# Expert-numbered blocks, early weight loads into slots of their own, and a permuted row order in a mixture-of-experts layer

## The chip, the cores and the metric

The kernel is one program on one core of a Trainium2 chip. The metric is device time in microseconds (us) for one execution; the smaller, the better.

## What is computed

One encoder layer on a sequence of 1024 tokens of width 1024, all in float32. A convolutional mixer comes first, then a mixture of experts (MoE) with 32 experts in 4 groups of 8. Each token takes the best group, then the two best experts in it, which makes 2048 pairs of token and expert. Cut to what matters here:

```python
order = jnp.argsort(expert)                      # 2048 pairs, sorted by expert
counts = jnp.bincount(expert, length=N_EXPERTS)
padded = ((counts + BLOCK_ROWS - 1) // BLOCK_ROWS) * BLOCK_ROWS     # BLOCK_ROWS = 128
...
def expert_block(args):
    xblk, e = args                               # 128 rows of width 1024
    a = xblk @ w_gate[e]                         # 1024 x 512
    u = xblk @ w_up[e]                           # 1024 x 512
    return (jax.nn.silu(a) * u) @ w_down[e]      # 512 x 1024
...
yb = yb * w_buf[:, None].astype(yb.dtype)
out = jnp.zeros_like(xt).at[tok_buf].add(yb)
```

With the inputs of the reference, the routing gives every expert between 10 and 130 tokens. One expert alone has more than 128, so there are 33 blocks, with 62 filled rows each on average.

## The kernel before

The engines run their own programs and meet at semaphores. TensorE (PE) multiplies. ScalarE (ACT) and VectorE (DVE) split each float32 operand into a high and a low part (`_hi`, `_lo`), and a product is three matmuls (`three`). GpSimd (POOL) issues the indirect transfers, and SyncE (SP) issues the weight loads.

**Routing.** After the output projection, DVE works out the experts, the weights, and for each pair its block and its row in the block. `posf` is the pair's place in the padded order. `blkf` is that place divided by 128 and `rowf` the rest. A one-hot product on PE (`inverse`, from `inv_b` and `oh_r`) turns this into the token of each row of each block, `idx_all`. `oh_r` compares `rowf` with `iota_r`, so partition p of a block holds row `iota_r[p]`, which is row p here. An unfilled row gets an index out of bounds, and the indirect transfers skip it. `tab` holds the expert of each block and the number of blocks, `n_blk`. `s_tab` says that `tab` is ready, and `s_pos` that `idx_all` is.

**Weights.** A block needs 6 chunks of 1024 KB: four of gate and up (a load of 512 KB of each, `load_gu`) and two of down (`load_down`). `e_raw`, `e_hi` and `e_lo` have one place for each of the six chunks. ACT rounds `e_raw` to `e_hi`, then DVE subtracts to get `e_lo` (semaphores `gu_lo`, `d_lo`), and then the place in `e_raw` is free for the next load. SP issues in this order: gate and up of block b+2, chunk by chunk as `gu_lo` of block b+1 arrives, then down of block b+1 as `d_lo` of block b arrives:

```python
e_gu = expert_of(b + 2)
for q in range(4):
    held(gu_lo, b * 4 + (4 + q + 1))
    load_gu(q, e_gu)
...
e_down = expert_of(b + 1)
for q in range(2):
    held(d_lo, b * 2 + (q + 1))
    load_down(q, e_down)
```

The loads of block 0 are issued behind the last matmul of the output projection (`pe_o`), and those of block 1 behind `s_tab`, the value that it gives, and `gu_lo` of block 0. A load has landed when its semaphore has had an increment from each of the DMA engines.

**A block.** POOL gathers the filled rows of the block from `d_h2` in HBM to `xg`, 4 KB each, two blocks ahead. PE transposes them, ACT and DVE split them (`xT_hi`, `xT_lo`), and PE multiplies by gate and up in 48 matmuls of 512 columns. ACT and DVE make `hid`, PE transposes it, and PE multiplies by down in 24 more matmuls. DVE scales the result to `y_sb` (L1389 in the profile, once a block). POOL adds the filled rows onto `d_x1` in HBM by an indirect transfer with accumulation (L632). The last two blocks go a way of their own, through a one-hot product and `f_x`.

**Tail.** SP loads `f_x`, DVE adds and norms, and the output is stored.

## Time and profile before

| what | before |
|---|---|
| median of 3 runs | 1692.61 us (1691.16 to 1692.96) |
| the profiled execution's own time | 1691.49 us |
| its span | 1689.8 us |
| mean granted clock of PE | 0.983 |
| busy: PE, PE weight load, DVE, ACT, POOL | 94%, 76%, 81%, 41%, 22% |
| moved by DMA | 351.83 MB, mean 208 GB/s |

The span is from the first to the last instruction of the profiled execution. The busy shares are means over stages that have different limits. From 1060.8 us to 1655.4 us the kernel is in the expert blocks, and what the change touches lies there and in the 80 us ahead of it. PE's busy time is modelled from pipelined matmuls, so an idle stretch of PE is surer than a busy one. The DMA share is the mean busy share of the 16 DMA engines.

### The profile page before, as it was taken

Reading aid. Unit: us, or ns where it says so; the run is one execution under the profiler, and the core shown is the slowest. Engines: PE = TensorE matmul, PEld = TensorE weight load, DVE = VectorE, ACT = ScalarE, POOL = GpSimd, SP = SyncE. Lnnn points to the kernel's source line nnn. Section 1 sums busy time; section 2 is a strip of 40 time slices with the busy share of each in tenths; the row PEclk is TensorE's granted clock in tenths of the full one; section 3 lists DMA queues with packets and bytes.
Section 4 is the critical chain, followed back from the end, with each engine's and each line's share of the span. In section 5 each row is a group of like instructions: output and inputs, shape, how many; then the busy total and the mean of one; then the engine's idle time right before and its main releaser. Section 6 shows DMA issues by size and latency. Waiting matters only on the chain.

```text
span 1689.8 us, 21438 instructions
## 1 busy us (share of the span) xinstructions
PE 1584.6 (94%) x7093; PEld 1291.7 (76%) x7093; DVE 1360.3 (81%) x1151; ACT 695.4 (41%) x584; POOL 365.5 (22%) x217
## 2 busy tenths in 40 slices
PE   2699999999999999999999988999999999999985
PEld 2588888888888888778878856888887777777774
DVE  5777878697878877988465467999999989989996
ACT  3411011211112012346131135777777666666773
POOL 1101000000000010000000011455454544445451
PEclk9999999999999999999999969999999999999997
DMA  7414233232314233535453248999999999999964
GB/s 251 151 63 137 63 111 105 73 120 87 112 62 137 58 116 114 179 118 187 140 174 138 87 175 310 367 364 372 377 357 351 355 359 358 356 351 359 371 198 163
DMA packets 167196, 351.83 MB, mean 208 GB/s; under 512 B 16907, under 2 KB 90659, under 8 KB 167158
## 3 DMA queue, kind: packets, MB, share of 16 engines
q1 hardware_dynamic: 150888, 309.73, 51.6%
q0 software_dynamic: 16272, 41.62, 8.1%
q8 instruction: 22, 0.36, 0.1%
q14 instruction: 14, 0.11, 0.0%
HBM read 323.32 MB, written 45.62 MB: 218 GB/s over the span
## 4 chain that ended last, share of the span: by engine, by line
PE 61%; DMA 16%; DVE 12%; issue 5%; ACT 3%; POOL 1%; DVEq 0%; SPq 0%; POOLq 0%; ACTq 0%
PE ps L1483 19%; PE ps L1485 19%; PE ps L1484 19%; DMA e_raw<-in_w_down_dram 12%; DMA xg<-d_h,g_idx 3%; DVE e_lo L1368 2%; DVE e_lo L1364 2%; ACT e_hi L854 2%; DVE conv_acc_b L1094 1%; DVE macc L1000 1%; PE ps L1703 1%; POOL g_idx L626 1%; PE ps L1636 1%; DVE B_lo L1179 1%; DMA prow<-in_c_dram 1%
## 5 line engine op out<-in xcount | busy, mean ns | idle before, releaser
L1483 PE MATMUL ps<-A_hi,w_hi 128*128 128x512 f32 x1024 | 400.7, 391 | 4.7 <-DVE A_lo L1030 4.7
L1485 PE MATMUL ps<-A_hi,w_lo 128*128 128x512 f32 x1024 | 399.3, 390 | 0.0
L1484 PE MATMUL ps<-A_lo,w_hi 128*128 128x512 f32 x1024 | 399.3, 390 | 0.0
L1364 DVE TENSOR_TENSOR e_lo<-e_raw,e_hi 128x2048 fp32r<-128x2048 f32 x136 | 309.1, 2286 | 11.5 <-ACT e_hi L848 9.9
L1094 DVE SCALAR_TENSOR_TENSOR conv_acc_b<-glu,colc,conv_acc_b 128x1024 f32<-128x1024 f32 x232 | 298.0, 1284 | 10.2 <-DVE rows L1079 0.5
L848 ACT CAST e_hi<-e_raw 128x2048 fp32r<-128x2048 f32 x136 | 259.7, 1913 | 61.3 <-PE ps L1485 56.6
L1483 PEld LDWEIGHTS ps<-A_hi,w_hi 128*128 128x128 f32 x1024 | 192.8, 188 | 46.0 <-issue 4.4
L1484 PEld LDWEIGHTS ps<-A_lo,w_hi 128*128 128x128 f32 x1024 | 192.8, 188 | 40.4 <-issue 0.5
L1485 PEld LDWEIGHTS ps<-A_hi,w_lo 128*128 128x128 f32 x1024 | 192.7, 188 | 40.2
L1483 PE MATMUL ps<-e_hi,xT_hi 128*128 128x512 f32 x528 | 212.5, 403 | 0.0
L1485 PE MATMUL ps<-e_hi,xT_lo 128*128 128x512 f32 x528 | 207.0, 392 | 0.0
L1484 PE MATMUL ps<-e_lo,xT_hi 128*128 128x512 f32 x528 | 206.3, 391 | 0.0
L1368 DVE TENSOR_TENSOR e_lo<-e_raw,e_hi 128x2048 fp32r<-128x2048 f32 x66 | 150.7, 2285 | 28.4 <-ACT e_hi L854 28.4
L854 ACT CAST e_hi<-e_raw 128x2048 fp32r<-128x2048 f32 x66 | 126.0, 1911 | 92.2 <-DMA e_raw<-in_w_down_dram 67.7
L632 POOL DMA_INDIRECT d_x<-y_sb,s_idx x31 | 86.4, 2786 | 297.2 <-DVE y_sb L1389 286.1
L970 DVE TENSOR_TENSOR w_lo<-w_raw,w_hi 128x1024 fp32r<-128x1024 f32 x72 | 87.9, 1222 | 63.9 <-ACT w_hi L711 60.4
L711 ACT CAST w_hi<-w_raw 128x1024 fp32r<-128x1024 f32 x72 | 73.6, 1047 | 156.8 <-PE ps L1485 154.0
L1483 PE MATMUL ps<-e_hi,hT_hi 128*128 128x512 f32 x264 | 106.6, 404 | 10.5 <-DVE hT_lo L1383 10.4
L1485 PEld LDWEIGHTS ps<-e_hi,xT_lo 128*128 128x128 f32 x528 | 99.4, 188 | 21.7
L1483 PEld LDWEIGHTS ps<-e_hi,xT_hi 128*128 128x128 f32 x528 | 100.1, 190 | 18.6
L1484 PEld LDWEIGHTS ps<-e_lo,xT_hi 128*128 128x128 f32 x528 | 99.7, 189 | 18.9
L1484 PE MATMUL ps<-e_lo,hT_hi 128*128 128x512 f32 x264 | 105.1, 398 | 0.0
(286 smaller groups left out, 2113.6 us busy)
## 6 DMA issues: line engine op xcount, KB each, us to landing
e_raw<-in_w_gate_dram SPq DMA_DIRECT2D x132, 512.0 KB, 6.0
e_raw<-in_w_up_dram SPq DMA_DIRECT2D x132, 512.0 KB, 12.5
e_raw<-in_w_down_dram SPq DMA_DIRECT2D x66, 1024.0 KB, 14.0
w_raw<-in_w_in_dram SPq DMA_DIRECT2D x56, 512.0 KB, 4.2
stream<-in_w_ada_dram SPq DMA_DIRECT2D x48, 512.0 KB, 5.6
xn<-in_x_dram SPq DMA_DIRECT2D x8, 512.0 KB, 6.5
d_short<-conv_acc_a POOLq DMA_DIRECT2D x8, 512.0 KB, 4.0
d_gate_a<-gate_st POOLq DMA_DIRECT2D x8, 512.0 KB, 2.9
```

What stands on the lines that cost most here:

```text
L626: g.tensor_copy(g_idx[:, slot:slot + 1], idx_all[:, bass.ds(blk, 1)]).then_inc(p_copy, 1)
L632: g.indirect_dma_start(d_x1, bass.IndirectOffsetOnAxis(ap=idx_ap, axis=0), rows_ap, None, bounds_check=S - 1, oob_is_err=False, compute_op ...
L711: a.copy(w_hi[:, slot, :], w_raw[:, slot, :]).then_inc(w_hi_done, 1)
L848: a.copy(e_hi[:, q, :], e_raw[:, q, :]).then_inc(gu_hi, 1)
L854: a.copy(e_hi[:, 4 + q, :], e_raw[:, 4 + q, :]).then_inc(d_hi, 1)
L970: v.tensor_tensor(w_lo[:, slot, :], w_raw[:, slot, :], w_hi[:, slot, :].bitcast(F32), ALU.subtract).then_inc(w_lo_done, 1)
L1094: lstep(v.scalar_tensor_tensor(conv_acc_b[:], glu[:, t:t + S], w, conv_acc_b[:], ALU.mult, ALU.add))
L1364: v.tensor_tensor(e_lo[:, q, :], e_raw[:, q, :], e_hi[:, q, :].bitcast(F32), ALU.subtract).then_inc(gu_lo, 1)
L1368: v.tensor_tensor(e_lo[:, 4 + q, :], e_raw[:, 4 + q, :], e_hi[:, 4 + q, :].bitcast(F32), ALU.subtract).then_inc(d_lo, 1)
L1483: t.matmul(dst, st_hi, mv_hi, start=first, stop=False)
L1484: t.matmul(dst, st_hi, mv_lo, start=False, stop=False)
L1485: return t.matmul(dst, st_lo, mv_hi, start=False, stop=last)
```

## The change

It has four parts.

1. **Block numbers.** Block e, for e from 0 to 31, is the first 128 rows of expert e. Rows past 128 of an expert go to blocks 32 and up. An expert's blocks past the first are now counted from `cmp_nb[:, 1:NT]`. `own` (the pair's expert) and the block past 32 make `blkf`. `n_blk` is 32 plus the blocks past the first, 33 as before for these inputs. DVE does more for this, in another order.
2. **Early weights.** Since blocks 0 to 31 need no table, SP issues gate and up of block 1 right behind block 0's, into four places of their own (`park`: the two down places of `e_hi`, one of `e_lo`, and two rows of `rows`). Gate and up of block 2 go to `e_raw` when block 0 has been split, and down of block 1 when block 0's has. The loop of SP starts at b = 1. ACT and DVE read block 1's chunks from `park`.
3. **Order on DVE.** The four splits of block 0 are no longer cut in two by `x_lo` of block 0.
4. **Row order.** `iota_r` is permuted. Partitions 0 to 3 hold rows 0, 16, 32 and 48, partitions 4 to 7 rows 1, 17, 33 and 49, and so on: partition 64h + 32a + 4b + c holds row 8h + 64a + b + 16c. Partitions 0 to 31 and 64 to 95 thus hold the first 64 rows.

The diff, cut to its core:

```diff
+        park = [at("park0", (NCH + 4) * 4 * C8, [P, C8], F32), at("park1", (NCH + 5) * 4 * C8, [P, C8], F32),
+                at("park2", (2 * NCH + 5) * 4 * C8, [P, C8], F32), at("park3", oR + SH2 * T4, [P, C8], F32)]
...
-            def load_gu(q, e):
+            def load_gu(q, e, parked=False):
                 for part, w in ((0, w_gate), (1, w_up)):
-                    dst = e_raw[:, q, part * D:(part + 1) * D].rearrange("p (k n) -> p k n", k=2)
+                    raw = park[q] if parked else e_raw[:, q, :]
+                    dst = raw[:, part * D:(part + 1) * D].rearrange("p (k n) -> p k n", k=2)
                     src = w[bass.ds(e, 1), 2 * q * P:2 * (q + 1) * P, :].rearrange("a (p k) n -> p (a k) n", p=P)
-                    sp.dma_start(dst, src).then_inc(e_full[q], 16)
+                    sp.dma_start(dst, src).then_inc((park_full if parked else e_full)[q], 16)
...
-            sp.wait_ge(s_tab, 1)
-            n_blk = sp.value_load(tab[0:1, NBLK:NBLK + 1], min_val=PAIRS // P, max_val=NBLK - 1)
-            e_one = sp.value_load(tab[0:1, 1:2], min_val=0, max_val=NE - 1)
+            for q in range(2):
+                load_gu(q, 1, True)
+            sp.wait_ge(s_h2, NT)
+            load_gu(3, 1, True)
+            sp.wait_ge(s_lgev, NT)
+            sp.wait_ge(sp_h2, 16 * NT)
+            load_gu(2, 1, True)
             for q in range(4):
                 sp.wait_ge(gu_lo, q + 1)
-                load_gu(q, e_one)
-            with sp.Fori(0, NBLK) as b:
+                load_gu(q, 2)
+            for q in range(2):
+                sp.wait_ge(d_lo, q + 1)
+                load_down(q, 1)
+            sp.wait_ge(s_tab, 1)
+            n_blk = sp.value_load(tab[0:1, NBLK:NBLK + 1], min_val=NE, max_val=NBLK - 1)
+            with sp.Fori(1, NBLK) as b:
...
-            g.iota(iota_r[:], pattern=[[1, P]], base=0, channel_multiplier=0, allow_small_or_imprecise_dtypes=True)
+            for half in range(2):
+                g.iota(iota_r[:, half * P // 2:(half + 1) * P // 2].rearrange("p (a b c) -> p a b c", a=2, b=8), pattern=[[P // 2, 2], [1, 8], [P // 8, 4]],
+                       base=half * 8, channel_multiplier=0, allow_small_or_imprecise_dtypes=True)
...
+            both = [P, 2, NT, NE]
+
+            def of_pair(dst, per_expert):
+
+                step(v.tensor_tensor(big[:], e_k[:], per_expert, ALU.mult))
+                step(v.tensor_reduce(dst, big[:], AX_X, ALU.add))
+
+            of_pair(own[:], bc(iota_n[:].unsqueeze(1), both))
...
-            step(v.tensor_reduce(nb_e[:], cmp_nb[:], AX_X, ALU.add))
+            step(v.tensor_reduce(nb_e[:], cmp_nb[:, 1:NT], AX_X, ALU.add))
...
+            rank = ps[:, 0, 0:NT * NE].rearrange("p (i e) -> p i e", i=NT)
+            of_pair(posf[:], bc(rank.unsqueeze(1), both))
+            step(v.tensor_copy(posi[:], posf[:]))
+            step(v.tensor_scalar(blk_i[:], posi[:], P.bit_length() - 1, None, ALU.arith_shift_right))
+            step(v.tensor_copy(blkf[:], blk_i[:]))
+            step(v.scalar_tensor_tensor(rowf[:], blkf[:], -float(P), posf[:], ALU.mult, ALU.add))
+            dve.wait_ge(h2_free, NT)
...
+            of_pair(posf[:], bc(cum[:, 0, :].unsqueeze(1).unsqueeze(1), both))
+            step(v.tensor_tensor(posf[:], posf[:], blkf[:], ALU.add))
+            step(v.scalar_tensor_tensor(posf[:], posf[:], float(NE - 1), own[:], ALU.add, ALU.subtract))
+            step(v.tensor_scalar(blkf[:], blkf[:], 1.0, None, ALU.min))
+            step(v.tensor_tensor(posf[:], posf[:], blkf[:], ALU.mult))
+            step(v.tensor_tensor(blkf[:], posf[:], own[:], ALU.add))
...
+            step(v.tensor_scalar(tab[:, NBLK:NBLK + 1], over, float(NE), None, ALU.add))
+            step(v.tensor_scalar(tab[:, NBLK + 1:NBLK + 2], over, float(NE - 1), None, ALU.add))
+            v.scalar_tensor_tensor(tab[:, 0:NBLK], ps[0:1, 1, H:H + NBLK], float(NE - 1), blk_own[0:1, :], ALU.min,
+                                   ALU.add).then_inc(s_tab, 1)
...
             n_blk = dve.value_load(tab[0:1, NBLK:NBLK + 1], min_val=PAIRS // P, max_val=NBLK - 1)
-            for q in range(2):
+            for q in range(4):
                 gu_split(q, q + 1)
             x_lo(0, 1)
-            for q in range(2, 4):
-                gu_split(q, q + 1)
 
             x_lo(1, 2, 1)
             for q in range(3):
-                gu_split(q, 4 + q + 1)
+                gu_split(q, 4 + q + 1, True)
             hidden(0, 1)
-            gu_split(3, 8)
+            gu_split(3, 8, True)
+            dve.wait_ge(gu_lo, 8)
```

The rows of `order` below name an instruction by its line, its operation and its tiles.

DVE between the counts of the experts and the first one-hot (`inv_b`), before. `nb_b` is what PE multiplies into the block starts, and `cum<-ps` reads them:

```order
L1309 TENSOR_TENSOR cnt_e<-ps,ident 32x1
...
L1312 TENSOR_SCALAR nb_b<-ones,nb_e 32x128
L1317 COPY cum<-ps 128x32
L1318 SCALAR_TENSOR_TENSOR mask<-cum,ps 128x256
L1321 TENSOR_TENSOR e_k<-e_k,mask 128x256
L1322 TENSOR_REDUCE posf<-e_k 128x8
...
L1323 CAST posi<-posf 128x16
L1326 TENSOR_SCALAR blk_i<-posi 128x16
L1327 CAST blkf<-blk_i 128x16
L1328 SCALAR_TENSOR_TENSOR rowf<-blkf,posf 128x16
L1330 TENSOR_TENSOR inv_b<-blk_no,blkf 128x8x48
```

The same place after the change:

```order
L1335 TENSOR_TENSOR big<-e_k,iota_n 128x512
L1336 TENSOR_REDUCE own<-big 128x16
L1340 TENSOR_TENSOR cnt_e<-ps,ident 32x1
...
L1343 TENSOR_SCALAR nb_b<-ones,nb_e 32x128
L1335 TENSOR_TENSOR big<-e_k,ps 128x512
L1336 TENSOR_REDUCE posf<-big 128x16
...
L1351 SCALAR_TENSOR_TENSOR rowf<-blkf,posf 128x16
L1356 COPY cum<-ps 128x32
L1335 TENSOR_TENSOR big<-e_k,cum 128x512
L1336 TENSOR_REDUCE posf<-big 128x16
L1358 TENSOR_TENSOR posf<-posf,blkf 128x16
...
L1362 TENSOR_TENSOR blkf<-posf,own 128x16
L1364 TENSOR_TENSOR inv_b<-blk_no,blkf 128x8x48
```

One pair of operations on 512 elements now stands ahead of `cnt_e`, one between `nb_b` and `cum<-ps`, and one behind it with five small operations.

SP, the weight loads from the last down chunk of block 0 to its loop, before:

```order
L475 DMA e_raw<-in_w_down_dram 128x2x1024 x2
L486 TENSOR_LOAD tab
...
L471 DMA e_raw<-in_w_gate_dram 128x1024
L471 DMA e_raw<-in_w_up_dram 128x1024
...
L491 UNCONDITIONAL_BRANCH
```

and after the change (`park_163` to `park_166` are the four places, chunks 0 to 3):

```order
L482 DMA e_raw<-in_w_down_dram 128x2x1024 x2
L478 DMA park_163<-in_w_gate_dram 128x1024
...
L478 DMA park_166<-in_w_gate_dram 128x1024
...
L478 DMA park_165<-in_w_gate_dram 128x1024
L478 DMA park_165<-in_w_up_dram 128x1024
L478 DMA e_raw<-in_w_gate_dram 128x1024
...
L482 DMA e_raw<-in_w_down_dram 128x2x1024 x2
L506 TENSOR_LOAD tab
```

The loads of block 1 moved ahead of the reading of the table, and those of block 2 and the down chunks of block 1 moved out of the loop and ahead of it too.

## Rows read from the trace of the kernel before

**Rows 1.** The page's slices of the span, 42.2 us each: DMA share and rate.

```profile
DMA  7414233232314233535453248999999999999964
GB/s 251 151 63 137 63 111 105 73 120 87 112 62 137 58 116 114 179 118 187 140 174 138 87 175 310 367 364 372 377 357 351 355 359 358 356 351 359 371 198 163
```

**Rows 2.** Busy time of each engine in stretches of the span.

```profile
core 0: us, PE busy (x) PEld busy (x) DVE busy (x) ACT busy (x) POOL busy (x), PEclk, DMA share, GB/s
980.00:990.00 10.00, 7.57 (x16) 3.66 (x16) 8.66 (x29) 1.63 (x3) 1.04 (x2) 0.50 1.01 404
...
994.00:1011.00 17.00, 12.09 (x46) 9.44 (x47) 11.75 (x36) 3.49 (x2) 0.00 (x0) 0.52 0.00 0
1011.00:1061.00 50.00, 41.97 (x177) 32.04 (x176) 40.21 (x24) 26.77 (x19) 8.52 (x7) 0.93 0.80 297
1060.00:1243.00 183.00, 182.12 (x846) 148.96 (x845) 176.58 (x111) 133.70 (x91) 95.56 (x40) 1.00 1.01 368
1243.00:1589.00 346.00, 329.50 (x1513) 265.73 (x1512) 316.31 (x200) 239.02 (x163) 161.36 (x72) 1.00 1.00 356
1589.00:1643.00 54.00, 51.91 (x240) 42.61 (x239) 52.94 (x34) 40.85 (x28) 30.73 (x13) 1.00 0.70 242
```

**Rows 3.** Line 1389, once a block, in three stretches; first and last start.

```profile
L1389 DVE SCALAR_TENSOR_TENSOR y_sb<-ps,w_all,rows x11: 1275/1278/1279, 1060.8 to 1243.3; 128x1024 f32<-128x1024 f32 x11
...
L1389 DVE SCALAR_TENSOR_TENSOR y_sb<-ps,w_all,rows x19: 1276/1278/1280, 1243.3 to 1588.9; 128x1024 f32<-128x1024 f32 x19
...
L1389 DVE SCALAR_TENSOR_TENSOR y_sb<-ps,w_all,rows x4: 1276/1277/1278, 1588.9 to 1642.9; 128x1024 f32<-128x1024 f32 x4
```

**Rows 4.** Waits, 1060 to 1240 us (first row), 1250 to 1590 us (others).

```profile
ACT e_hi L854 <- DMA e_raw<-in_w_down_dram: 3.8, 3, 1.4
...
ACT e_hi L854 <- DMA e_raw<-in_w_down_dram: 61.5, 33, 3.6
...
PE ps L1703 <- DMA xg<-d_h,g_idx: 11.6, 15, 1.3
```

**Rows 5.** Median time from issue to landing, 1050 to 1160, then 1250 to 1400 us.

```profile
e_raw<-in_w_down_dram SPq DMA_DIRECT2D x12, 1024.0 KB, 9.9
...
e_raw<-in_w_down_dram SPq DMA_DIRECT2D x16, 1024.0 KB, 14.6
```

**Rows 6.** The page: GpSimd's queue (packets, MB, share of 16 engines), and DMA issues.

```profile
q0 software_dynamic: 16272, 41.62, 8.1%
...
e_raw<-in_w_up_dram SPq DMA_DIRECT2D x132, 512.0 KB, 12.5
e_raw<-in_w_down_dram SPq DMA_DIRECT2D x66, 1024.0 KB, 14.0
...
d_short<-conv_acc_a POOLq DMA_DIRECT2D x8, 512.0 KB, 4.0
```

**Rows 7.** Timeline of DVE, 988 to 1003 us: start, duration, idle before in brackets.

```profile
988.65 0.88 DVE L1295 TENSOR_TENSOR e_k<-oh_g,oh_k 128x256 f32<-128x256 f32 x2 [0.15 <-DVE gsm L1291]
...
994.29 0.15 DVE L1309 TENSOR_TENSOR cnt_e<-ps,ident 32x1 f32<-32x1 f32 x1 [1.41 <-PE ps L1675]
...
995.97 0.19 DVE L1317 COPY cum<-ps 128x32 f32<-128x32 f32 x1 [0.78 <-PE ps L1678]
...
999.31 0.56 DVE L1330 TENSOR_TENSOR inv_b<-blk_no,blkf 128x384 f32<-128x384 f32 x1
...
1001.08 1.22 DVE L1334 TENSOR_TENSOR oh_r<-iota_r,rowf 128x1024 f32<-128x1024 f32 x1
```

**Rows 8.** Timelines of PE and of ACT at the start of the blocks.

```profile
1023.24 1.98 PE L1703 MATMUL ps<-ident,xg 128*128 128x128 f32 x8 [1.88 <-DMA xg<-d_h,idx_all]
...
1029.18 1.91 ACT L848 CAST e_hi<-e_raw 128x2048 fp32r<-128x2048 f32 x1 [2.91 <-PE ps L1485]
```

**Rows 9.** Timeline of POOL where it makes its constants, 880 to 886 us.

```profile
881.79 0.24 POOL L598 IOTA iota_r<- 128x128 f32 x1
...
885.11 0.55 POOL L607 DMA_DIRECT2D d_x<-stream  x1 [2.80 <-DVE stream L1234]
```

More of the change, by code:

```diff
@@ L186, in encoder_block @@
         blk_no = rt("blk_no", [P, NBLK])
+        blk_over = rt("blk_over", [P, NBLK])
+        blk_own = rt("blk_own", [P, NBLK])
+        iota_n = rt("iota_n", [P, NT, NE])
         gsm = rt("gsm", [P, 8, NT])
@@ L205, in encoder_block @@
         blk_i = rt("blk_i", [P, 2, NT], I32)
+        own = rt("own", [P, 2, NT])
         blkf = rt("blkf", [P, 2, NT])
@@ L208, in encoder_block @@
         tok1 = rt("tok1", [P, NT])
-        inv_b = rt("inv_b", [P, 2, NT, 2, NBLK])
         oh_r = at("oh_r", oW, [P, 2, NT, P], F32)
         iota_r = rt("iota_r", [P, P])
+        inv_b = rt("inv_b", [P, 2, NT, 2, NBLK])
         no_row = rt("no_row", [P, NBLK])
@@ L512, in _ @@
             sp.wait_ge(s_oht, 4)
-            sp.dma_start(rows[:, SH2, :], g_final.partition_broadcast(P).rearrange("p a n -> p (a n)")).then_inc(s_g2_in, 16)
+            sp.dma_start(rows[:, GT1, :], g_final.partition_broadcast(P).rearrange("p a n -> p (a n)")).then_inc(s_g2_in, 16)
             for i in range(NT):
@@ L684, in _ @@
                 pool.wait_ge(f_norm, n + 1)
-                g.tensor_tensor(f_o[:, i, :], f_n[:, n % 2, :], rows[:, SH2, :], ALU.mult).then_inc(f_outp, 1)
+                g.tensor_tensor(f_o[:, i, :], f_n[:, n % 2, :], rows[:, GT1, :], ALU.mult).then_inc(f_outp, 1)
         @block.scalar
@@ L1317, in _ @@
             step(v.tensor_copy(cum[:, 0, :], ps[:, 3, 0:NE]))
-            step(v.scalar_tensor_tensor(mask[:], bc(cum[:, 0, :].unsqueeze(1), [P, NT, NE]), float(P),
-                                        ps[:, 0, 0:NT * NE].rearrange("p (i e) -> p i e", i=NT), ALU.mult, ALU.add))
-            for k in range(2):
-                step(v.tensor_tensor(e_k[:, k], e_k[:, k], mask[:], ALU.mult))
-                step(v.tensor_reduce(posf[:, k, :], e_k[:, k], AX_X, ALU.add))
-            step(v.tensor_copy(posi[:], posf[:]))
-            dve.wait_ge(h2_free, NT)
-            step(v.tensor_scalar(blk_i[:], posi[:], P.bit_length() - 1, None, ALU.arith_shift_right))
-            step(v.tensor_copy(blkf[:], blk_i[:]))
-            step(v.scalar_tensor_tensor(rowf[:], blkf[:], -float(P), posf[:], ALU.mult, ALU.add))
+            of_pair(posf[:], bc(cum[:, 0, :].unsqueeze(1).unsqueeze(1), both))
[4 more added lines that the diff above has]
+            step(v.tensor_tensor(blkf[:], posf[:], own[:], ALU.add))
             for k in range(2):
@@ L1463, in final @@
                     if i not in POOL_TILES:
-                        v.scalar_tensor_tensor(f_o[:, i, :], f_x[:, i, :], rstd[:, i:i + 1], rows[:, SH2, :],
+                        v.scalar_tensor_tensor(f_o[:, i, :], f_x[:, i, :], rstd[:, i:i + 1], rows[:, GT1, :],
                                                ALU.mult, ALU.mult).then_inc(f_out, 1)
```

47 lines of the change are left out of this document (25 added, 22 removed).

## Prediction

> **What bounds the kernel now.** I read the slices first. From slice 26 to 38 the DMA share stands at its top digit and the rate at 351 to 377 GB/s, with no great rise or fall [rows 1]. That covers the expert blocks, and it does not say who waits for whom. The stretches do [rows 2]. From 1060 to 1243 us PE is busy 182.12 of 183 us, so PE sets the pace there, although the DMA share reads 1.01. From 1243 to 1589 us it is busy 329.50 of 346 us, while the rate has gone down from 368 to 356 GB/s at the same share. The line that ends a block shows the pace [rows 3]: (1243.3 - 1060.8)/10 = 18.25 us a block, then (1588.9 - 1243.3)/18 = 19.20 us, then (1642.9 - 1588.9)/3 = 18.0 us.
>
> The waits name what changed [rows 4]. ACT waits for the down chunks 3.8 us in the first stretch and 61.5 us in the second. A down load takes 9.9 us to land early and 14.6 us later [rows 5]. So the weight stream runs a little slower than PE from the start. It lives on a reserve of some 5 to 8 us in the time to landing, which ten blocks eat up at about 1 us a block. From then on the stream is the bound.
>
> What makes the stream slow? A block's weights are 4 x 2 x 512 KB and 2 x 1024 KB, that is 6.29 MB [rows 6]. At the 404 GB/s that the same loads reach at 980 to 990 us [rows 2] they need 15.6 us. The rest of the 19.2 us is 3.6 us for 62 rows of 4 KB in and as many out. These are 0.51 MB, 1.3 us at that rate when all 16 engines share them equally. GpSimd's queue took 8.1% of 16 engines' span, 8.1% x 16 x 1689.8 = 2190 us of engine time, for 41.62 MB [rows 6]. Of these, 48 plain stores of 512 KB (six groups of eight, one of which is shown) are 25.2 MB, 997 us at 404/16 GB/s for each engine. That leaves 1193 us, or 36 us for each of 33 blocks. Over 16 engines it is 2.3 us, over 8 engines 4.5 us. So a block costs 17.8 us on every engine if the rows are spread evenly, and 20.1 us on the loaded ones if half of the engines carry them. The measured 19.2 us is nearer to the second. Filled rows lie in partitions 0 to 61 on average, half of the 128, so I take it that half of the engines carry them and that every weight load, which needs its last engine, waits for these.
>
> No row tells the engine of a packet. The Trainium skill ("DMA: Bandwidth & Descriptors", The descriptor swizzle) gives engine = 8 x (partition >> 6) + ((partition >> 2) & 7) for a transfer over 128 partitions. By it, partitions 0 to 63 are engines 0 to 7, and the new order puts row r on engine r mod 16; that no row here can show, and 19.2 us agrees with it.
>
> **The change, part by part.**
>
> *Row order.* The same rows now load all engines. With the 3.6 us as the pace of eight loaded engines, the rows are 29 us of engine time, 1.8 us on each of 16, and a block's stream takes 15.6 + 1.8 = 17.4 us. The bound from the queue's share is 17.8 us. Both are under PE's 18.25 us, so the weights should leave the path and the 18 slow blocks should run at 18.25 us: 18 x 0.95 = 17.1 us gained. The first ten and the last three blocks gain nothing, since PE holds them already. As a check, the idle time of PE from 1243 to 1643 us is 16.5 + 2.1 = 18.6 us, of which 1.9 us stay at the first stretch's 0.5%: 16.7 us. The margin of 0.45 to 0.85 us a block is thin, and blocks are unequal (10 to 128 rows). I leave 1.0 us of waits standing. If the margin is not there, the price is 0.1 us x 18 for each 0.1 us above 18.25, after the reserve is gone.
>
> *Early weights.* The DMA engines are idle from 994 to 1011 us (share 0.00) and at 0.80 from 1011 to 1061 us [rows 2]. Four MB of block 1 move into the first gap. But nobody waited for them: at 1029.18 us, when ACT begins with block 1, it has waited for PE [rows 8]. The gain can only be a larger reserve for later. At block 1 the reserve is nearly whole already, since a down load takes 9.9 us in the median of the first six blocks. Bounds: 0 at one end, and at the other the transfer of 4.19 MB at 356 GB/s, 11.8 us, if the stream were the bound without a break from 1033 us on. Where the row order takes the stream off the path, it is 0, which I take. Where it doesn't, I take 1.9 us, two blocks at the 0.95 us by which the slow ones are slower: nearer to 0, since the reserve is used up only some ten blocks later.
>
> *Routing on DVE.* The edits from `cnt_e` to `inv_b` are on the path, for PE waits for the one-hots. An operation on 256 elements takes 0.44, on 384 elements 0.56 and on 1024 elements 1.22 us [rows 7]. So one on 512 is about 0.70, and a pair is 1.4 us. The first pair (`own`) goes into the 1.41 us in which DVE waited for the counts: nothing. Without that cover it would cost 1.4 us. Then from the end of `nb_b`, before: 0.78 us of waiting, and 3.34 us from `cum` at 995.97 to `inv_b` at 999.31, together 4.1 us. After: 1.4 + four small operations at 0.2 + `cum` 0.2 + 1.4 + five small 1.0 = 4.9 us. The block starts have arrived by then. The sum is +0.8 us, and `s_tab` and `s_pos` move with it. Behind them stand the gathers, SP's table and every engine's `n_blk`.
>
> *First gathers.* PE starts block 0 after the rows of block 1, for which it waits 1.88 us until 1023.24 us [rows 8]. With the rows spread, these gathers should land somewhat sooner, beside 2 MB of weight loads as before. Bounds 0 and 1.0 us; I take 0.5 us, half of it, since I have no row of a spread gather.
>
> *POOL's constants.* Five more small operations (`iota_r` is made in two halves) come between 881.79 and 885.11 us. At the 0.24 us of `iota_r` they are some 1.2 us in all, and POOL has 2.80 us there [rows 9]: nothing. Four splits of block 0 in a row on DVE: PE reads them later than DVE ends them in both orders, nothing. DVE's and ACT's added waits are for their own or finished work, nothing. The number of blocks stays 33, and the tail after 1643 us is the same work.
>
> **Sum,** against the profiled execution's own 1691.49 us: -17.1 + 1.0 + 0.8 - 0.5 = -15.8, so 1675.7 us. The median of the runs is 1.1 us above that execution, which makes 1676.8 us; I say 1677.
>
> **Rivals.**
>
> 1. *The stream stays the bound, halfway.* The share reads 1.00 to 1.01 in both stretches [rows 2], as if all 16 engines were busy and none had room for the others' rows. For it: that reading. Against it: at the same share the rate is 404, 368 and 356 GB/s, so the share does not tell work from standing in line. If the evened pace is 18.7 us, half of the gain is left: 18 x 0.5 = 9.0 and 1.9 from the early weights, less 0.3 of routing and gathers and 2 for unequal blocks: 8.6 us, about 1684 us.
> 2. *The rows cost what they cost on any engine, or the partitions are dealt to engines in another way than I take.* Then the new order changes nothing, the late blocks stay at 19.2 us, and the early weights give 1.9 us, less 0.3 us of routing and gathers: 1691 us. For it: the share again, and no row with an engine's number. Against it: 3.6 us for what at an even deal costs 1.3 to 2.3 us. The Trainium skill (same page, Specifications) gives about 358 GB/s as HBM's limit for one core, which speaks against this change: by it 356 GB/s is the end and 1691 us the outcome. The trace does not agree, with 368 GB/s over 183 us and 404 GB/s over 10 us.
> 3. *Slower: sixteen late engines instead of eight.* Each load waits for its last engine. If scattering with accumulation holds up whichever engine it is on, all 16 now have it, and the last of 16 is later than the last of 8, from the first block on. At 19.2 us for all 31 periods the first ten cost 9.5 us more: 1692.6 + 9.5 + 0.3 = 1702 us. It decides from a mean period of 18.8 us on. For it: the longest wait ends with a load, not a row. Against it: the work on each engine halves, and the first ten blocks already run at 18.25 us with such scatters. The Trainium skill (same page, Latency and other measured facts) says that engines 7 and 15 are usually slower than the others; engine 15 would now get rows as well. No run here shows engines apart.
>
> **How the numbers follow.** My forecast has 0.66, rival 1 has 0.16, rival 2 has 0.12, rival 3 has 0.06. The forecast's own range is 1672 us (gathers and PE's waits fully gained) to 1680 us (pace 18.4 us). With rival 1 and the near edge of rival 2 the range is 1671 to 1690 us. A change under 0.2%, 3.4 us, is about what a measurement of this kernel can't tell from none. Rival 2 falls within it, with a part of rival 1's upper end: faster 0.83, same 0.11, slower 0.06.
>
> **What the changed kernel's profile would show.** The line that ends a block comes every 18.2 to 18.4 us throughout, also from 1243 us on. ACT's wait for down chunks stays under 15 us over all blocks, and the time to landing stays near 10 us. PE is busy over 98% from 1060 to 1620 us. `inv_b` starts 0.8 us later. There is a burst of DMA between 994 and 1011 us, and the first matmul of block 0 starts at 1025 us as before. I am wrong if the late blocks keep 19.2 us (rival 2) or stop between (rival 1), or if the first ten lose their 18.25 us (rival 3).

## The result, and the profile after

The changed kernel takes 1670.7 us (median of 4 runs, 1668.35 to 1673.36), the kernel before on the same chip 1692.78 us (4 runs, 1691.16 to 1694.01). The ratio is 0.9871 with a 95% interval from 0.9854 to 0.9888: 22.1 us faster. The forecast was 1677.0 us in a range from 1671 to 1690. The direction was right, and the time is 6.3 us below the forecast and 0.3 us below the range. The profiled execution took 1670.95 us, with a span of 1669.3 us, against 1691.49 and 1689.8 us.

From the page of the changed kernel: the slices of the span (41.7 us each), GpSimd's queue and the issues of the weight loads, as in [rows 1] and [rows 6].

```profile
DMA  7414133232323142544544273999999999999964
GB/s 254 153 64 137 50 127 97 79 113 95 116 66 113 63 139 54 198 151 139 172 155 156 101 288 140 329 369 394 374 358 391 377 373 368 378 386 382 375 195 167
q0 software_dynamic: 16272, 41.88, 8.3%
e_raw<-in_w_down_dram SPq DMA_DIRECT2D x66, 1024.0 KB, 7.6
e_raw<-in_w_up_dram SPq DMA_DIRECT2D x128, 512.0 KB, 7.1
```

The same work of GpSimd's queue is there (16272 packets, and its share is about the same), yet the weights land in 7.6 and 7.1 us where it was 14.0 and 12.5 us [rows 6]. The rate in the expert blocks is 358 to 394 GB/s, where it was 351 to 377 [rows 1].

Busy time of the engines in the stretches of [rows 2], for the changed kernel:

```profile
core 0: us, PE busy (x) PEld busy (x) DVE busy (x) ACT busy (x) POOL busy (x), PEclk, DMA share, GB/s
980.00:990.00 10.00, 7.08 (x16) 3.20 (x15) 8.63 (x30) 1.69 (x3) 1.29 (x2) 0.62 1.02 412
994.00:1011.00 17.00, 11.06 (x45) 9.04 (x45) 12.79 (x38) 3.44 (x2) 0.00 (x0) 0.50 0.55 220
1011.00:1061.00 50.00, 43.32 (x172) 32.27 (x172) 40.24 (x26) 25.41 (x18) 6.99 (x7) 0.91 0.58 215
1060.00:1243.00 183.00, 183.00 (x860) 151.57 (x859) 178.84 (x113) 136.38 (x92) 93.83 (x40) 1.00 1.00 371
1243.00:1589.00 346.00, 343.95 (x1601) 282.55 (x1600) 335.37 (x210) 253.73 (x171) 181.34 (x76) 1.00 1.01 377
```

The early weights show as a share of 0.55 from 994 to 1011 us, where the DMA engines were idle. From 1243 to 1589 us PE is idle for 2.05 us instead of 16.5. The DMA share reads 1.01 there at 377 GB/s, where it read 1.00 at 356 [rows 2]: the share is the same, and the bytes are 6% more.

The line that ends a block (1425 now, 1389 before), over the same blocks as in [rows 3]:

```profile
L1425 DVE SCALAR_TENSOR_TENSOR y_sb<-ps,w_all,rows x11: 1276/1278/1279, 1061.6 to 1241.7; 128x1024 f32<-128x1024 f32 x11
...
L1425 DVE SCALAR_TENSOR_TENSOR y_sb<-ps,w_all,rows x19: 1276/1277/1278, 1241.7 to 1568.6; 128x1024 f32<-128x1024 f32 x19
...
L1425 DVE SCALAR_TENSOR_TENSOR y_sb<-ps,w_all,rows x4: 1276/1276/1278, 1568.6 to 1622.9; 128x1024 f32<-128x1024 f32 x4
```

That is 18.01 us a block for the first ten (before 18.25), 18.16 us for the next 18 (before 19.20) and 18.1 us for the last three (before 18.0).

The waits from 1243 to 1589 us hold no down chunk any more, against 61.5 us in [rows 4]. What is left for a transfer is this row, 11.6 us before:

```profile
PE ps L1738 <- DMA xg<-d_h,g_idx: 2.0, 6, 0.6
```

The routing on DVE, for the rows of [rows 7]:

```profile
992.73 0.69 DVE L1335 TENSOR_TENSOR big<-e_k,iota_n 128x512 f32<-128x512 f32 x1
993.46 0.69 DVE L1336 TENSOR_REDUCE own<-big 128x16 f32<-128x512 f32 x1
994.24 0.14 DVE L1340 TENSOR_TENSOR cnt_e<-ps,ident 32x1 f32<-32x1 f32 x1
...
997.55 0.19 DVE L1356 COPY cum<-ps 128x32 f32<-128x32 f32 x1
...
1000.27 0.56 DVE L1364 TENSOR_TENSOR inv_b<-blk_no,blkf 128x384 f32<-128x384 f32 x1
```

The pair for `own` lies where DVE waited 1.41 us for the counts, and `cnt_e` starts at 994.24 us as before (994.29). `inv_b` starts at 1000.27 instead of 999.31 us.

The starts of PE and ACT that answer to [rows 8]:

```profile
1023.33 1.98 PE L1738 MATMUL ps<-ident,xg 128*128 128x128 f32 x8 [1.94 <-DMA xg<-d_h,idx_all]
```

```profile
1028.91 1.91 ACT L870 CAST e_hi<-park 128x2048 fp32r<-128x2048 f32 x1 [2.55 <-PE ps L1520]
```

PE waits for the rows of block 1 as it did, 1.94 us, and is 0.1 us later although the routing is 1.0 us later.

### The profile page after: what moved, and what is told of

The parts are those of the page before. It is cut to its first block, busy times and chain, and to the rows that moved or that the text cites. A ratio compares the mean times of both kernels' runs of the same rounds, so it can differ in the third digit from the quotient of the medians.

```text
span 1669.3 us, 21394 instructions
## 1 busy us (share of the span) xinstructions
PE 1580.0 (95%) x7093; PEld 1293.9 (78%) x7093; DVE 1364.7 (82%) x1157; ACT 697.0 (42%) x584; POOL 374.5 (22%) x222
## 3 DMA queue, kind: packets, MB, share of 16 engines
q0 software_dynamic: 16272, 41.88, 8.3%
## 4 chain that ended last, share of the span: by engine, by line
PE 80%; DVE 8%; issue 4%; DMA 4%; ACT 2%; POOL 1%; DVEq 0%; POOLq 0%; SPq 0%; ACTq 0%
PE ps L1518 25%; PE ps L1520 25%; PE ps L1519 25%; DMA xg<-d_h,g_idx 3%; PE ps L1738 2%; DVE macc L1023 1%; ACT e_hi L870 1%; DVE e_lo L1400 1%; POOL g_idx L648 1%; PE ps L1743 1%; PE ps L1671 1%; DVE B_lo L1202 1%; DMA prow<-in_c_dram 0%; DVE xnT L1010 0%; PE ps L1720 0%
## 5 line engine op out<-in xcount | busy, mean ns | idle before, releaser
L1400 DVE TENSOR_TENSOR e_lo<-e_raw,e_hi 128x2048 fp32r<-128x2048 f32 x132 | 301.2, 2287 | 15.4 <-ACT e_hi L870 14.2
L870 ACT CAST e_hi<-e_raw 128x2048 fp32r<-128x2048 f32 x132 | 251.9, 1912 | 80.5 <-PE ps L1520 80.5
L1404 DVE TENSOR_TENSOR e_lo<-e_raw,e_hi 128x2048 fp32r<-128x2048 f32 x66 | 150.6, 2283 | 0.9 <-ACT e_hi L876 0.9
L876 ACT CAST e_hi<-e_raw 128x2048 fp32r<-128x2048 f32 x66 | 126.1, 1913 | 47.7 <-PE ps L1520 47.7
L1520 PE MATMUL ps<-e_hi,hT_lo 128*128 128x512 f32 x264 | 105.5, 400 | 0.0
```

The costliest lines, as they stand in the source:

```text
L870: a.copy(e_hi[:, q, :], park[q][:] if parked else e_raw[:, q, :]).then_inc(gu_hi, 1)
L876: a.copy(e_hi[:, 4 + q, :], e_raw[:, 4 + q, :]).then_inc(d_hi, 1)
L1400: v.tensor_tensor(e_lo[:, q, :], park[q][:] if parked else e_raw[:, q, :], e_hi[:, q, :].bitcast(F32), ALU.subtract).then_inc(gu_lo, 1)
L1404: v.tensor_tensor(e_lo[:, 4 + q, :], e_raw[:, 4 + q, :], e_hi[:, 4 + q, :].bitcast(F32), ALU.subtract).then_inc(d_lo, 1)
L1520: return t.matmul(dst, st_lo, mv_hi, start=False, stop=last)
```

## The experiments

Two theories were to be told apart first. Theory A: the rows' place is the whole gain, because the weight stream leaves the path; the early weights add nothing. Theory B: the early weights are part of it. When the first runs had answered that, the size of the gain and the first ten blocks were still open.

All runs, with the ratio to the kernel before on the same chip. A block's time is the distance of the starts of the line that ends a block, as in [rows 3], for the first ten, the next 18 and the last three. The measurement tells 0.2% (3.4 us) from no change.

| run | us, median | ratio, 95% interval | us a block |
|---|---|---|---|
| before | 1692.8 | 1 | 18.25, 19.20, 18.0 |
| after | 1670.7 | 0.9871 [0.9854, 0.9888] | 18.01, 18.16, 18.1 |
| e1 rows only | 1670.07 | 0.987 [0.9855, 0.9885] | 18.11, 18.04, 18.0 |
| e2 early weights only | 1693.57 | 1.0013 [1.0004, 1.0022] | 18.27, 19.19, 17.7 |
| e3 even engines | 1679.8 | 0.9935 [0.9917, 0.9953] | 18.12, 18.54, 17.7 |
| e8 odd engines | 1681.64 | 0.9941 [0.9917, 0.9964] | 18.28, 18.58, 17.7 |
| e9 pairs in both halves | 1682.05 | 0.9943 [0.9928, 0.9959] | 18.11, 18.59, 17.7 |
| e10 upper half | 1692.94 | 1.0008 [0.9997, 1.0019] | 18.22, 19.12, 18.0 |
| e4 before, half of the down bytes | 1679.11 | 0.9932 [0.9913, 0.995] | 18.32, 18.42, 18.1 |
| e7 e4 and gather first | 1667.17 | 0.9859 [0.9835, 0.9883] | 17.97, 17.93, 17.9 |
| e6 before and gather first | 1689.76 | 0.9992 [0.998, 1.0004] | 18.25, 19.23, 17.7 |
| e5 after and gather first | 1667.07 | 0.9855 [0.9832, 0.9877] | 17.96, 17.93, 17.9 |
| e11 rows only and gather first | 1665.59 | 0.9841 [0.9827, 0.9854] | 17.97, 17.93, 17.9 |

### One part at a time: rows only (e1), early weights only (e2)

e1 is the kernel before with one edit, e2 the changed kernel with this edit undone.

```diff
-            g.iota(iota_r[:], pattern=[[1, P]], base=0, channel_multiplier=0, allow_small_or_imprecise_dtypes=True)
+            for half in range(2):
+                g.iota(iota_r[:, half * P // 2:(half + 1) * P // 2].rearrange("p (a b c) -> p a b c", a=2, b=8), pattern=[[P // 2, 2], [1, 8], [P // 8, 4]],
+                       base=half * 8, channel_multiplier=0, allow_small_or_imprecise_dtypes=True)
```

> The kernel before with the new row order alone: block numbers, early weights and DVE's routing as before. Theory A (the spread rows are the whole gain, the rest costs about 0.8 us of routing): 1669 to 1673 us, blocks at 18.0 us early and 18.2 us late, like the changed kernel or up to 1 us better. Theory B (the early weights give a reserve that the spread alone lacks): 1675 to 1683 us, late blocks at 18.5 us or more. Theory C (the early weights are the gain): 1690 us or more.

> The changed kernel with the old row order (partition p holds row p): early weights and expert-numbered blocks alone. Theory A: 1690 to 1694 us, early blocks at 18.2 us, late ones at 19.2 us. Theory B: the larger reserve puts off the slow stretch by a few blocks, 1684 to 1689 us. Theory C: 1671 to 1676 us.

e1 took 1670.07 us, what the changed kernel takes. Its waits from 1243 to 1589 us hold no down chunk, and this row is what is left for a transfer:

```profile
PE ps L1705 <- DMA xg<-d_h,g_idx: 0.7, 3, 0.3
```

e2 took 1693.57 us, nothing gained and, by its interval, 0.04 to 0.22% lost, which has room for the routing's 1 us. In the profile of e2 the down chunks are waited for as before, and a little more than before:

```profile
ACT e_hi L874 <- DMA e_raw<-in_w_down_dram: 66.4, 35, 4.0
```

So one table of 128 numbers is the gain. And the 4 MB in the gap, with the new numbers of the blocks that make them possible, bring nothing that can be told from noise, with spread rows and without.

### Is it the load on each engine? Four other placements (e3, e8, e9, e10)

Each has other numbers in `iota_r`, with all the rest of the changed kernel. The engines named are by a rule of the Trainium skill ("DMA: Bandwidth & Descriptors", The descriptor swizzle), which deals the partitions in groups of four, 0 to 63 to engines 0 to 7 and 64 to 127 to engines 8 to 15. No run here shows an engine's number.

In this order, e3 (partition 8m + s holds row m + 16s: the even engines), e8 (rows 0 to 63 in every second group of four partitions: the odd engines) and e10 (rows 0 to 63 in partitions 64 to 127):

```diff
+            g.iota(iota_r[:].rearrange("p (m s) -> p m s", s=8), pattern=[[1, 16], [16, 8]], base=0, channel_multiplier=0,
+                   allow_small_or_imprecise_dtypes=True)
...
+            for s in range(2):
+                g.iota(iota_r[:].rearrange("p (m s c) -> p m s c", m=16, s=2)[:, :, s, :], pattern=[[1, 16], [16, 4]], base=64 * (1 - s),
+                       channel_multiplier=0, allow_small_or_imprecise_dtypes=True)
...
+            g.iota(iota_r[:, 0:P // 2], pattern=[[1, P // 2]], base=P // 2, channel_multiplier=0, allow_small_or_imprecise_dtypes=True)
+            g.iota(iota_r[:, P // 2:P], pattern=[[1, P // 2]], base=0, channel_multiplier=0, allow_small_or_imprecise_dtypes=True)
```

e9 (adjacent pairs of engines in both halves):

```diff
+            for h in range(2):
+                for a_ in range(2):
+                    for y in range(2):
+                        part = iota_r[:, h * 64 + a_ * 32:h * 64 + a_ * 32 + 32].rearrange("p (x y z) -> p x y z", x=2, y=2)
+                        g.iota(part[:, :, y, :].rearrange("p x (z c) -> p x z c", z=2), pattern=[[2, 2], [1, 2], [8, 4]],
+                               base=64 * y + 4 * h + 32 * a_, channel_multiplier=0, allow_small_or_imprecise_dtypes=True)
```

It puts rows 0 to 63 into the first eight of every 16 partitions: 0-7, 16-23, 32-39 and so on to 112-119. By the rule these are the engines that the expectation below names, 0, 1, 4, 5, 8, 9, 12 and 13; the partitions that it names are wrong.

> The changed kernel with another permuted order: partition 8m+s holds row m+16s, so a block of 64 rows fills partitions 0-3 of each group of 8. If an engine serves 8 neighbouring partitions (0 to 7, 8 to 15, ...), this spreads rows over all 16 engines and gives 1670 us like the changed kernel. If an engine serves two groups of 4 neighbours, 32 apart, as the Trainium skill (DMA: Bandwidth & Descriptors, The descriptor swizzle) has it, the rows again lie on 8 engines, and it gives 1688 to 1694 us with late blocks at 19.2 us. If it is not about engines at all but about any permutation of partitions, 1670 us.

> The changed kernel with another row order: rows 0 to 63 in partitions 4-7, 12-15, 20-23 and so on, the other half of each group of eight. By the Trainium skill (DMA: Bandwidth & Descriptors, The descriptor swizzle) these are engines 1, 3, 5 to 15, where the order that gave 1679.8 us used engines 0, 2, 4 to 14. Theory P (it matters how the eight engines are spread over the sixteen): 1678 to 1682 us again. Theory S (it matters whether one of two slower engines, 7 and 15, carries rows): 1688 to 1694 us, as with the old order, which has engine 7 among its eight.

> The changed kernel with other numbers in iota_r alone: a block's first 64 rows stand in partitions 0-15, 32-47, 64-79 and 96-111, by the page's rule on engines 0, 1, 4, 5, 8, 9, 12, 13: eight engines again, in adjacent pairs, but half of them in each half of the sixteen. Both earlier placements on every other engine (one on the even, one on the odd ones) took some 1680-1682 us, the placement on engines 0-7 took 1693.6. Theory N (engines 2k and 2k+1 share something, so that two loaded neighbours hold each other up): as on engines 0-7, 1690 to 1694 us, slow blocks at 19.2. Theory H (it matters that rows load one half of the engines, 0-7, and not the other): as every other engine, 1678 to 1683 us, slow blocks at 18.5. In between would mean that neither alone is the cause.

> The changed kernel with iota_r turned by 64: a block's first 64 rows stand in partitions 64-127, by the page's rule on engines 8-15 alone. Theories N (neighbours) and H (one half of the sixteen) both expect the time of the old order: 1690 to 1695 us, slow blocks at 19.2. If engines 0-7 had other work besides (small loads, stores of few rows) that made them the late ones, these engines would be better: under 1688 us. If engine 15 were slow, worse: over 1697 us.

e3 fitted none of its expectations, and e8 was made for the first explanation of that, which fell: the odd engines, 7 and 15 among them, take 1681.64 us, where the even ones take 1679.8. The Trainium skill (same page, Latency and other measured facts) says that 7 and 15 are usually the slow ones; no run here shows it. e9 and e10 then separated neighbours from halves. Eight loaded engines in one half cost 1693 us, lower or upper alike; in e10 ACT's waits for down chunks are nearly those of before:

```profile
ACT e_hi L875 <- DMA e_raw<-in_w_down_dram: 57.3, 33, 3.7
```

Eight loaded engines in both halves cost 1680 to 1682 us, neighbours or not. All sixteen cost 1670.

Two things outside of the profile's own views, taken from its record of each engine's completions, show what happens. "spread" is the time from the eighth to the last of the 16 engines' completions of a block's first down chunk:

```
us from block to block, blocks 1 to 31
before 17.7 18.8 18.0 18.5 18.1 17.9 18.1 18.2 18.3 19.0 19.1 19.3 19.5 17.5 19.2 19.5 19.4 18.8 19.9 18.8 20.7 18.3 20.3 19.2 19.4 18.6 19.2 18.9 17.8 18.4 17.8
e3     18.5 18.2 17.9 18.2 17.9 17.9 18.3 18.3 18.0 17.9 17.9 18.0 18.1 18.2 18.3 18.7 18.1 18.3 18.3 18.3 18.8 20.0 18.3 19.9 18.4 17.5 18.9 19.8 17.5 17.7 17.9
after  18.2 17.9 18.1 17.9 17.9 17.9 18.2 17.9 17.9 17.9 17.9 17.9 18.0 18.0 17.9 17.9 17.9 18.5 18.9 18.5 18.2 18.5 17.9 18.4 18.2 17.9 18.3 17.9 18.5 17.9 17.9
spread, us, blocks 0 to 30
before 1.2 1.7 1.6 1.0 2.1 4.3 3.9 3.7 5.9 6.1 7.0 8.8 9.4 9.3 10.2 7.4 8.5 9.6 10.0 8.5 9.1 9.2 11.3 9.0 10.6 9.6 9.5 8.8 9.1 8.8 5.9
e3     1.5 0.2 0.3 0.9 2.0 2.2 3.0 4.0 2.9 3.3 1.8 1.5 1.8 4.7 4.9 3.4 3.6 5.0 4.5 5.7 5.1 7.2 8.0 9.4 8.3 8.6 8.6 7.0 7.1 9.6 5.8
after  1.4 0.3 0.3 1.1 0.5 2.3 2.7 2.4 1.2 2.1 1.4 1.8 1.3 2.3 1.2 0.6 1.6 1.2 1.8 1.2 1.0 1.6 1.7 2.8 1.8 1.8 1.1 0.8 0.7 2.1 2.7
```

Before, the last engine falls behind from block 5 on until it is some 9 us behind the eighth, where it stays. From then on the blocks take 19.2 us. In e3 the same happens at about half the speed, so that its last blocks are nearly as slow as those of before, and fewer. After, the last stays within 3 us of the eighth. All 16 completions tell how many engines are late:

```
us behind the first engine, in the order in which they end: first down chunk, mean of blocks 20 to 28
before 0.0 0.0 0.1 0.1 0.2 0.2 0.3 0.4 0.8 0.9 1.5 1.7 2.2 2.9 5.2 10.0
e10    0.0 0.0 0.1 0.2 0.2 0.2 0.3 0.8 1.1 1.3 1.5 1.9 2.2 2.6 6.3 10.0
e3     0.0 0.0 0.1 0.1 0.2 0.3 0.4 1.0 2.6 2.8 3.3 3.5 6.8 7.8 8.1 8.7
e8     0.0 0.1 0.1 0.2 0.3 0.4 0.5 0.9 2.3 2.4 2.8 3.0 3.3 5.9 8.7 9.1
e9     0.0 0.1 0.1 0.2 0.3 0.4 0.5 0.8 2.3 2.4 2.5 3.6 4.9 5.5 7.8 9.0
after  0.0 0.1 0.2 0.2 0.3 0.3 0.4 0.5 0.7 0.8 1.0 1.2 1.3 1.5 1.8 1.9
```

Before and in e10 one engine is far behind and a second half as far. In e8 two or three are late, in e3 and e9 four. It is never eight alike.

So the load on each engine decides, as the prediction took it. Placements on eight engines differ by 11 to 13 us, and it looks as if the eight of one half shared something. But e3, e8 and e9 differ from before and e10 in a second thing, which none of the expectations reckons with: how evenly the eight are loaded. Blocks are unequal, and in the order of before and e10 a block is filled from its first partition on, so a block of 33 rows gives engine 0 five rows and engines 1 to 7 four each. e3, e8 and e9 deal the rows to their engines in turn. From the counts of the experts in the reference's inputs (33, 34, 66, 111 rows in the first four blocks) and the rule above, the rows of the most loaded engine over all 33 blocks are these:

| placement | most loaded | the next three | us |
|---|---|---|---|
| before, e2; e10 (8 to 15) | 237 | 228, 222, 216 | 1692.8, 1693.57; 1692.94 |
| e3, e8 | 221 | 217, 214, 212 | 1679.8, 1681.64 |
| e9 | 218 | 215, 211, 208 | 1682.05 |
| after, e1 | 145 | 141, 138, 136 | 1670.7, 1670.07 |

It fits that before and e10 have one engine far behind, with 9 rows more than the next, and that e3, e8 and e9 have two to four close together, with 9 or 10 rows between the first and the fourth, where before has 21. As an estimate, the prediction's 1193 us of engine time for 2048 rows in and out is 0.58 us a row, so 16 to 19 rows more on the engine that every load waits for are 9 to 11 us, of the 11 to 13 measured. That leaves little or nothing for something shared by the engines of a half. It is argued and not shown: no run deals the rows in turn to the engines of one half.

### How fast without the stream? Half of the down bytes (e4, e7)

```diff
-                src = w_down[bass.ds(e, 1), 2 * q * P:2 * (q + 1) * P, :].rearrange("a (k p) n -> p (a k) n", p=P)
-                sp.dma_start(e_raw[:, 4 + q, :].rearrange("p (k n) -> p k n", k=2), src).then_inc(e_full[4 + q], 16)
+                n_k = 2 if isinstance(e, int) else 1
+                src = w_down[bass.ds(e, 1), 2 * q * P:(2 * q + n_k) * P, :].rearrange("a (k p) n -> p (a k) n", p=P)
+                sp.dma_start(e_raw[:, 4 + q, 0:n_k * D].rearrange("p (k n) -> p k n", k=n_k), src).then_inc(e_full[4 + q], 16)
```

This is the kernel before with the second half of each down chunk left out from block 1 on. It computes with a stale half. A block's weights are 5.24 MB instead of 6.29.

> The kernel before, with only the first half of each down chunk loaded from block 1 on (512 instead of 1024 KB; the other half keeps old data, so the second half of each down product is left to stale weights). All instructions stay. It takes 1 MB of 6.3 MB a block from the stream. Theory A (18.25 us in the first ten blocks was not PE's own pace, the stream cost something there too): all blocks at 17.9 to 18.0 us, 1662 to 1672 us. Rival (18.25 us is PE's pace): first ten blocks stay at 18.2 to 18.3 us, and the rest come down to that, 1674 to 1677 us.

e4 took 1679.11 us: more than the changed kernel with all of its bytes, which no theory expected. Its profile has no wait for weights, and the DMA share has room for the first time:

```profile
1060.00:1243.00 183.00, 180.59 (x842) 148.52 (x842) 176.10 (x111) 133.65 (x90) 93.81 (x40) 1.00 0.89 306
1243.00:1589.00 346.00, 340.40 (x1582) 278.80 (x1581) 331.26 (x207) 251.04 (x170) 169.27 (x76) 1.00 0.92 315
```

The waits of that run from 1243 to 1589 us that have to do with the rows' transposes:

```profile
PEld ps L1704 <- issue: 11.0, 13, 1.3
PE ps L1704 <- DMA xg<-d_h,g_idx: 5.3, 8, 0.9
```

So with the stream out of the way there was a second thing at 18.3 to 18.4 us a block, and it is not PE's own work. The gathers were the suspects. In the kernel before, a gather is one link of a ring. POOL from 1148 us on:

```profile
1171.84 2.80 POOL L632 DMA_INDIRECT d_x<-y_sb,s_idx  x1 [7.76 <-DVE y_sb L1389]
1174.09 2.43 POOL L626 COPY g_idx<-idx_all 128x1 int32 x1
1177.37 2.50 POOL L628 DMA_INDIRECT xg<-d_h,g_idx  x1 [0.85 <-POOL g_idx L626]
...
1189.97 2.79 POOL L632 DMA_INDIRECT d_x<-y_sb,s_idx  x1 [7.77 <-DVE y_sb L1389]
```

DVE and PE in the same blocks of that kernel:

```profile
1169.68 1.28 DVE L1389 SCALAR_TENSOR_TENSOR y_sb<-ps,w_all,rows 128x1024 f32<-128x1024 f32 x1
...
1187.80 1.27 DVE L1389 SCALAR_TENSOR_TENSOR y_sb<-ps,w_all,rows 128x1024 f32<-128x1024 f32 x1
```

```profile
1167.99 1.22 PE L1703 MATMUL ps<-ident,xg 128*128 128x128 f32 x8
...
1186.21 1.22 PE L1703 MATMUL ps<-ident,xg 128*128 128x128 f32 x8
```

The `y_sb` at 1169.68 ends the block that PE has left just before the transposes at 1167.99. From it to the scatter's issue at 1171.84 is 2.16 us, to the gather's issue at 1177.37 5.53 us, and the rows land 8.84 us later, when the next transposes begin at 1186.21: 16.53 us. The ring closes through the block that the transposes at 1167.99 open: its `y_sb` comes 19.81 us after them, at 1187.80. That is 36.3 us for two blocks, 18.2 us each, where PE's own work takes 17.93 (e7 below). The median time to landing of the ten gathers from 1060 to 1240 us is 8.8 us before and 8.1 us after:

```profile
DMA to landing us min/median/max: 8.4/8.8/8.9
```

```profile
DMA to landing us min/median/max: 7.8/8.1/8.5
```

From 1250 us on it is 8.5 us in both, before (first row) and after (second row), so how long a gather takes isn't a matter of its rows' place alone:

```profile
DMA to landing us min/median/max: 7.6/8.5/9.0
...
DMA to landing us min/median/max: 7.8/8.5/9.6
```

### Taking the ring apart (e5, e6, e7)

POOL issues the gather of block b + 3 before the scatter of block b - 1, not after it that of b + 2. It is the same number of gathers, each most of a block earlier.

```diff
             g.tensor_copy(s_idx[:, 0:1], idx_all[:, 0:1]).then_inc(p_copy, 1)
             pool.wait_ge(p_copy, 5)
+            pool.wait_ge(t_done, 3)
+            gather(0, 4, 6)
...
-                            held(t_done, b + 1)
-                            gather(slot, b + 2, b * 2 + 2)
+                            held(t_done, b + 2)
+                            gather(1 - slot, b + 3, b * 2 + 3)
...
-                            held(p_copy, b * 2 + 3)
+                            held(p_copy, b * 2 + 4)
```

> The changed kernel, with GpSimd issuing the gather of block b+3 ahead of the scatter of block b-1 instead of the gather of block b+2 behind it, so that a gather no longer stands behind the end of a block (y_sb) and the scatter. Theory A (in the changed kernel the gather's round trip of scatter, copy, gather and landing is about as long as PE's turn and adds the rest of the waits): PE's waits for xg gone, blocks at 17.9 us throughout, 1664 to 1668 us. Rival (the remaining 18.2 us in the middle blocks is the weight stream or DVE): no change within 2 us, 1669 to 1672 us.

> The kernel before with the same exchange of gather and scatter, and nothing else. Theory A (the first ten blocks were held at 18.25 us by the gather's round trip, the middle ones at 19.2 us by DVE's waits for down chunks): first ten blocks at 17.9 to 18.0 us, middle ones at 19.1 us or more, 1686 to 1691 us. Rival (the gather's round trip is what passes the late weights on to PE in the middle blocks too): middle blocks under 18.6 us, 1675 to 1682 us.

> The kernel before with half of each down chunk loaded from block 1 on (the other half keeps stale weights) and with the gather ahead of the scatter. Theory A (with half of the down bytes the 18.4 us of a block were the gather's round trip): all blocks at 17.9 to 18.0 us, 1660 to 1668 us. Rival (the 18.4 us were something else of the stream): 1675 to 1680 us as without the exchange.

e5 took 1667.07 us, and each block from the second on takes 17.9 us. Its profile has PE busy without a gap over both stretches:

```profile
1060.00:1243.00 183.00, 183.00 (x861) 152.05 (x860) 178.30 (x112) 136.33 (x92) 93.40 (x40) 1.00 1.00 369
1243.00:1589.00 346.00, 346.00 (x1623) 287.21 (x1622) 339.30 (x213) 257.46 (x175) 179.76 (x78) 1.00 1.02 381
```

e7, which is e4 with this edit, has the same 17.93 us a block:

```profile
1243.00:1589.00 346.00, 346.00 (x1623) 287.21 (x1622) 339.36 (x213) 257.39 (x174) 180.39 (x78) 1.00 0.93 322
```

With fewer bytes and with all of them, that is PE's own pace. The 18.4 us of e4 was the ring. On the kernel before (e6) the edit gives no change that can be told (0.998 to 1.0004). Its second to sixth blocks come at 17.9 us, so the reserve is gone by block 7 and not by block 10, and the rest is at the stream's 19.23 us. ACT's waits for down chunks in its first stretch:

```profile
ACT e_hi L856 <- DMA e_raw<-in_w_down_dram: 15.0, 10, 2.6
```

### The two edits that count, alone (e11)

e11 is the kernel before with the spread `iota_r` and the gather first, nothing else.

> The kernel before with two edits: iota_r in the spread order, and POOL issues the gather of block b+3 ahead of the scatter of block b-1. No early weights, no new numbers of blocks. If the early weights and the routing that they need are worth nothing (theory A, and what the run with the spread rows alone showed), it takes what the changed kernel with the exchange took, less the 0.8 us of routing: 1665 to 1668 us, 17.93 to 18.0 us a block throughout. Theory B, that a reserve of weights is worth something once PE runs at its own pace: 1670 us or more, with waits for down chunks in the first blocks.

It took 1665.59 us, 0.9841 of before: the lowest of all, with 17.93 us a block in the middle, and simpler than the changed kernel. It is 1.5 us under e5, too little to tell by itself.

## Why the prediction came out as it did

By its own steps, with the distances in the two profiled executions:

| term | forecast, us | measured, us |
|---|---|---|
| routing and first gathers (first `y_sb` 1060.8 to 1061.6) | +0.8 - 0.5 | +0.8 |
| first ten blocks (182.5 to 180.1) | 0 | -2.4 |
| next 18 blocks (345.6 to 326.9) | -17.1 + 1.0 | -18.7 |
| last three blocks (54.0 to 54.3) | 0 | +0.3 |
| from the last `y_sb` to the end (46.9 to 46.4) | 0 | -0.5 |
| sum (the spans, 1689.8 to 1669.3) | -15.8 | -20.5 |

- **The stream was the bound in the late blocks, and spreading the rows takes it off the path:** right, and shown by e1 and e2. The waits for down chunks went from 61.5 us to none listed, the time to landing from 14.0 to 7.6 us.
- **Half of the engines carry the rows:** right in the main. e10 puts them on the other half and takes the old time, and eight engines in both halves are in between. By the counts and the rule of e3 to e10, engines 0 to 7 get 1666 of the 2048 rows. But the prediction loads them alike (36 us a block over 8 is its 4.5 us), and the completions show one engine far behind and not eight.
- **Early weights 0 where the rows are spread:** right (e1 beside the changed kernel). Where they are not, I had put 1.9 us, in rivals 1 and 2. That was wrong: e2 gained nothing.
- **Routing +0.8:** `inv_b` is 0.96 us later. The pair over 512 elements took 0.69 and 0.69 us, as worked out, and the first pair lay in its cover. The prediction's terms from `nb_b` on add up to 4.8 us and not 4.9, so it had 0.7 us.
- **First gathers -0.5:** PE's transposes went from 1023.24 to 1023.33 us against a routing 0.96 us later, so 0.9 us, near the upper bound. That this comes from the spread rows is not shown: the first two gathers landed after 7.3 and 7.8 us before and 6.6 and 6.9 us after, but after 8.4 and 8.5 us in e1, which has the spread rows too. And block 0 didn't keep it: the first `y_sb` is 0.8 us later. That row of the table is within what varies anyway, for e4 and e6, whose routing and block 0 are those of before, have their first `y_sb` at 1062.0 and 1060.4 us.
- **The step that failed** is "From 1060 to 1243 us PE is busy 182.12 of 183 us, so PE sets the pace there", and with it "the 18 slow blocks should run at 18.25 us" and "The first ten and the last three blocks gain nothing, since PE holds them already". PE's own pace is 17.93 us (e5, e7, e11). The first ten blocks were held at 18.25 us in part by the ring through POOL, whose gather landed in 8.8 us, and in 8.1 us after. The term for these ten blocks, put at 0, was 2.4 us. In the sum, 18.01 for 18.25 us is 2.4 us in the first ten, and 18.16 for 18.25 is 1.6 us in the next 18. The 1.0 us that I left standing for unequal blocks did not come on top: these waits are within the 18.16. So the terms for both stretches were 5.0 us too small (2.4 + 2.6), and the rest 0.3 us too favourable, which makes the 4.7 us between the sums. The other 1.6 us of the 6.3 are the median's place beside the profiled execution, 1.1 us above it before and 0.25 us below it after, and my rounding.
- **The range** missed by 0.3 us, less than the runs of one kernel differ by (1668.35 to 1673.36 us), so that alone says little; the mis-sized step is seen in the distances of the blocks. It missed for the same reason: its lower end took 18.25 us as the floor of a block. With 17.93 us for all 31 blocks the gain has its bound at 582.1 - 31 x 17.93 = 26.3 us, some 1666 us, and the lower end belonged there; e11 took 1665.59 us.
- **Rivals.** 1 (stream stays the bound, halfway) did not come: e3, e8 and e9 look like it, with eight loaded engines, and the changed kernel does not. 2 fell with e1. The limit of 358 GB/s that it names (the Trainium skill, "DMA: Bandwidth & Descriptors", Specifications) does not agree with 377 GB/s over 346 us after, nor with 381 in e5. 3 (sixteen late engines) fell too: the last engine is within 3 us of the eighth throughout. Its 1702 us leave out the last three blocks, which at 19.2 us would add 3.6 us.

What is open: whether the uneven load on one half's engines is all of the 11 to 13 us between the placements; and how much of the 2.4 us in the first ten blocks is the gather's 0.7 us and how much the stream's. e6, with the ring taken apart and the rows on eight engines, has 17.9 us in five of its first six blocks, and e4, with the ring and a sixth of the stream left out, has 18.32 us in its first ten. Both speak for the ring there. With the rows alone (e1) the first ten take 18.11 us and not 18.01.
